# Pair sums of the hidden activations made in place from two loaded blocks, and ten weight sums moved to the second gate loop

## The reference, cut to what matters

```python
# first block, phase E of the kernel
f = (silu(h @ w_ffn_gate) * (h @ w_ffn_up)) @ w_ffn_down
x = x + rms_norm(f, norm_ffn_post)
# second block, phase H of the kernel
h = x @ w_up                      # 1024 x 5632
h = causal_conv3(h, conv_w) + conv_b
a, g = split(h, 2)
out = (silu(g) * a) @ w_down      # then residual and the final norm
```

## Time and profile before

| what | us |
|---|---|
| median of three runs | 3157.57 |
| lowest and highest run | 3152.23, 3159.49 |
| the profiled execution | 3161.4 |
| its span | 3159.7 |
| PE busy | 2939.5 (93%) |
| DVE busy | 1897.9 (60%) |
| ACT busy | 1315.3 (42%) |
| POOL busy | 725.5 (23%) |

### The profile page before, as it was taken

The page is one execution under the profiler, slowest core; times in us unless marked ns, Lnnn a source line. Parts: engine busy times, 40 slices in busy tenths (PEclk is TensorE's granted clock), DMA queues, the critical chain, the costliest instruction groups (busy, mean ns, idle before and its releaser), DMA issues.

```text
span 3159.7 us, 41058 instructions
## 1 busy us (share of the span) xinstructions
PE 2939.5 (93%) x14905; PEld 2400.7 (76%) x14905; DVE 1897.9 (60%) x2684; ACT 1315.3 (42%) x2136; POOL 725.5 (23%) x645
## 2 busy tenths in 40 slices
PE   8989999999989798999999999999979899988898
PEld 6767778778868576788777887788867677767687
DVE  3546565565675647666556574555744776777656
ACT  3531441541542435233224453555644444333444
POOL 3211121221231301334662001333510000243200
PEclk8999999999999999999999999999989999999999
DMA  4256356356342562555458564557663344556765
GB/s 138 71 155 141 122 145 160 99 147 149 97 123 61 194 227 80 144 160 139 144 159 285 181 220 137 142 184 183 172 203 135 101 114 115 163 152 199 250 200 194
DMA packets 330037, 488.32 MB, mean 155 GB/s; under 512 B 18818, under 2 KB 214160, under 8 KB 329888
## 3 DMA queue, kind: packets, MB, share of 16 engines
q1 hardware_dynamic: 276064, 298.16, 30.3%
q0 software_dynamic: 48016, 171.37, 20.1%
q10 hardware_dynamic: 5808, 16.79, 1.8%
HBM read 379.24 MB, written 199.29 MB: 183 GB/s over the span
## 4 chain that ended last, share of the span: by engine, by line
PE 66%; DVE 13%; DMA 8%; ACT 6%; issue 3%; POOL 3%; SPq 1%; DVEq 0%; ACTq 0%; POOLq 0%
PE PS L671 19%; PE PS L2528 15%; PE PS L2548 12%; PE PS L377 5%; PE PS L1504 2%; DMA pair_hidden<-hidden_scratch 1%; DVE gate_up L2422 1%; PE PS L1470 1%; PE PS L1398 1%; DMA down_raw<-up_sums 1%; PE PS L1387 1%; DVE w_L L2374 1%; DMA sb_branch<-u_scratch 1%; PE PS L3218 1%; PE PS L3205 1%
## 5 line engine op out<-in xcount | busy, mean ns | idle before, releaser
L671 PE MATMUL PS<-hH,w_H 128*128 128x512 f32 x1072 | 453.5, 423 | 22.8 <-DVE w_L L334 12.5
L671 PE MATMUL PS<-hH,w_L 128*128 128x512 f32 x1072 | 426.2, 398 | 0.0
L671 PE MATMUL PS<-hL,w_H 128*128 128x512 f32 x1072 | 424.3, 396 | 0.0
L334 DVE TENSOR_TENSOR w_L<-w_raw,w_H 128x1024 fp32r<-128x1024 f32 x107 | 133.7, 1250 | 218.6 <-ACT w_H L329 218.4
L671 PEld LDWEIGHTS PS<-hH,w_H 128*128 128x128 f32 x1072 | 207.1, 193 | 68.4 <-issue 12.3
L2528 PE MATMUL PS<-hH,fast_w 128*128 128x512 f32 x672 | 232.6, 407 | 23.6 <-ACT gate_up L2300 21.2
L671 PEld LDWEIGHTS PS<-hH,w_L 128*128 128x128 f32 x1072 | 204.9, 191 | 46.6
L671 PEld LDWEIGHTS PS<-hL,w_H 128*128 128x128 f32 x1072 | 206.4, 193 | 35.8 <-issue 1.7
L2528 PE MATMUL PS<-sums,w_H 128*128 128x512 f32 x672 | 212.3, 398 | 8.4 <-DVE gate_up L2422 8.2
L2528 PEld LDWEIGHTS PS<-hH,fast_w 128*128 128x128 f32 x672 | 129.5, 193 | 61.8 <-ACT gate_up L2300 25.0
L2824 POOL TENSOR_SCALAR prob<-prob,den_inverse 128x128 f32<-128x128 f32 (+3 forms) x64 | 110.3, 1723 | 234.0 <-DVE den_inverse L3034 233.7
(11 more groups left out here) (477 smaller groups left out, 6758.6 us busy)
## 6 DMA issues: line engine op xcount, KB each, us to landing
up_sums<-in_w_up POOLq DMA_DIRECT2D x24, 1408.0 KB, 10.3
w_raw<-in_w_in SPq DMA_DIRECT2D x62, 512.0 KB, 4.6
u_scratch<-unit_staged SPq DMA_DIRECT2D x50, 512.5 KB, 5.2
hidden_scratch<-hidden SPq DMA_DIRECT2D x44, 512.0 KB, 5.0
pair_sums<-pair_sum POOLq DMA_DIRECT2D x22, 1024.0 KB, 5.6
turned_raw<-pair_sums SPq DMA_DIRECT2D x88, 256.0 KB, 3.0
turned_raw<-down_sums SPq DMA_DIRECT2D x88, 256.0 KB, 4.1
down_raw<-up_sums SPq DMA_DIRECT2D x42, 512.0 KB, 6.6
```

The lines of the kernel that those rows point to most:

```text
L334: e.tensor_tensor(wL[c % 2][:, :, :], raw[c % 2][:, :, :], f32(wH[c % 2][:, :, :]), ALU.subtract).then_inc(s_wL, 1)
L671: mm = e.matmul(PS[:, f.bank(o, half), :], w[:, k0 + k, :], x[:, k, half * HALF:(half + 1) * HALF], start=(k == 0 and j == 0), stop=(k == ...
```

## The change

**Pair sums.** POOL no longer reads `hidden`. It waits until tile 11 + p is stored, loads both tiles p and 11 + p from DRAM into `pair_sum`, one turn later makes the four sums there in place, in a chain in which each waits for the one before, and stores all 2048 columns. The order of the four in the buffer differs, so `DOWN_A` names them in another order. The waits of ACT (`up_start`) and DVE (`tile_hidden`) on `pair_summed` are gone. The memory of `pair_hidden` stays as a pad.

**Order on POOL.** In a turn of the second half POOL now does: the sums of the pair before, then the wait for the next weights, the store of the pair, (in E) the four weight sums, and then the two loads of the next pair. Before it was: wait for the weights, store, load, (E) weight sums, pair sums.

**Slots of the down loop.** The first nine steps take slots 0, 1, 2, 9, 10, 7, 3, 4, 5 (before 0, 1, 2, 9, 10, 3, 4, 5, 6) and the ring of nine behind them runs in another order, so that the slot in `silu_out` and `hidden` is first used at step 13 (before 8) and that in `pair_sum` at step 17 (before 10). The store of the last `hidden` tile is issued behind the load of step 11 (before 8). The check that tiles are stored moves from step 11 to steps 20 and 21.

**Weight sums in DRAM.** F now issues 5 of the 64 parts (before 16), G 3, and the last 10 are issued in the first eleven turns of H's gate loop.

```diff
-                ("pair_loaded", "EH", 16 * NG), ("pair_summed", "EH", 8 * NG), ("pair_stored", "EH", 16 * NG),
+                ("pair_loaded", "EH", 32 * NG), ("pair_summed", "EH", 4 * NG), ("pair_stored", "EH", 16 * NG),
...
-        DOWN_A = ((HIDDEN, 0, 0), (HIDDEN, NG, 0), (SUMS, 1), (SUMS, 0), (SUMS, 3), (SUMS, 2), (HIDDEN, NG, 1))
+        DOWN_A = ((HIDDEN, 0, 0), (HIDDEN, NG, 0), (SUMS, 0), (SUMS, 3), (SUMS, 2), (SUMS, 1), (HIDDEN, NG, 1))
...
-        slot_no = lambda n: (0, 1, 2, NSLOT, NSLOT + 1)[n] if n < 5 else (n - 2) % NSLOT
+        SLOT_FIRST, SLOT_RING = (0, 1, 2, NSLOT, NSLOT + 1, 7, 3, 4, 5), (0, 1, 2, 7, 6, 3, 4, 5, 8)
+        slot_no = lambda n: SLOT_FIRST[n] if n < NSLOT else SLOT_RING[(n - NSLOT) % NSLOT]
...
-            if n == NG:
-                e.wait_ge(sem("fast_stored"), since(tag, "fast_stored", 16 * FT))
+            if n in (2 * NG - 2, 2 * NG - 1):
+                e.wait_ge(sem("fast_stored"), since(tag, "fast_stored", 16 * (n + 1)))
...
-            elif n in (5, 6):
+            elif n == 5:
+                e.wait_ge(sem("down_L"), since(tag, "down_L", 6))
+            elif n in (6, 7):
                 e.wait_ge(sem("fast_P"), since(tag, "fast_P", 7 * NW))
-            elif n == 7:
+            elif n == 8:
                 e.wait_ge(sem("hidden"), since(tag, "hidden", FT))
-            elif n == 8:
+            elif n == 13:
                 e.wait_ge(sem("fast_stored"), since(tag, "fast_stored", 16 * FT))
-                e.wait_ge(sem("pair_summed"), since(tag, "pair_summed", 8 * NG))
-            elif n == 9:
-                e.wait_ge(sem("pair_summed"), since(tag, "pair_summed", 8 * NG))
-                e.wait_ge(sem("down_L"), since(tag, "down_L", 6))
-            elif n == 10:
+            elif n == 17:
                 e.wait_ge(sem("pair_stored"), since(tag, "pair_stored", 16 * NG))
...
-                if n == 8:
+                if n == 11:
                     store(None, NW, FT - 1)
...
+            def pair_sums(p):
+                e.wait_ge(sem("pair_loaded"), since(tag, "pair_loaded", 32 * p + 32))
                 summed = sem("pair_summed")
+                done = lambda n: e.wait_ge(summed, since(tag, "pair_summed", 4 * p + n))
+                a_lo, a_hi, b_lo, b_hi = (pair_sum[:, i, :] for i in range(4))
+                e.tensor_tensor(b_hi, a_hi, b_hi, ALU.subtract).then_inc(summed, 1)
                 done(1)
+                e.tensor_tensor(a_hi, a_lo, a_hi, ALU.subtract).then_inc(summed, 1)
                 done(2)
+                e.tensor_tensor(a_lo, a_lo, b_hi, ALU.subtract).then_inc(summed, 1)
+                done(3)
+                e.tensor_tensor(b_lo, b_lo, a_lo, ALU.subtract).then_inc(summed, 1)
...
+            def pair_load(p):
+                e.wait_ge(sem("fast_stored"), since(tag, "fast_stored", 16 * (NG + p + 1)))
+                if p:
+                    e.wait_ge(sem("pair_stored"), since(tag, "pair_stored", 16 * p))
+                for i in range(2):
+                    e.dma_start(pair_sum[:, 2 * i:2 * i + 2, :], h_scr[:, i * NG + p, :].rearrange("p (n c) -> p n c", n=2))\
+                        .then_inc(sem("pair_loaded"), 16)
...
             for t in range(NW):
+                if t > NG:
+                    pair_sums(t - NG - 1)
                 if t < NW - 1:
                     tile_loaded(t + 2)
-                if t < NG and tag == "E":
+                if t < NG:
                     weight_sums_next(parts, 1)
-                if t == NG:
-                    e.wait_ge(sem("hidden"), since(tag, "hidden", 2))
                 if t > NG:
-                    pair_store(t - 1)
-                if t >= NG:
-                    pair_load(t)
+                    pair_store(t - NG - 1)
                 if tag == "E" and t < NW - 1:
                     weight_sums(1, t)
                 if t >= NG:
-                    pair_sums(t)
+                    pair_load(t - NG)
...
@@ up_start (ACT, H) and tile_hidden (DVE, E)
-                e.wait_ge(sem("pair_summed"), own("pair_summed", tag, 4 * c + 3, it, 4))
...
@@ pool_F
-                if G % 4 == 2:
+                if G % 13 == 6:
                     weight_sums_next(parts, 1)
@@ pool_H
+            pool_ffn(e, "H", "G", UH, parts)
             assert next(parts, e) is e
-            pool_ffn(e, "H", "G", UH, parts)
```

More of the change, by code:

```diff
@@ L272, in build @@
                 op_pair = sb("down_operands_pair", [P, 8, HALF], F32R, s1)
-            pair_sum, pair_h, raw_first = T("pair_sum", (P, 4, HALF)), T("pair_hidden"), T("down_raw_first", (P, 2, HALF))
+            pair_sum, pad_E, raw_first = T("pair_sum", (P, 4, HALF)), T("pad_e"), T("down_raw_first", (P, 2, HALF))
             cvt = T("conv_columns", (P, 16))
@@ L2178, in pair_sums @@
                 summed = sem("pair_summed")
-                done = lambda n: e.wait_ge(summed, own("pair_summed", tag, n, it, 4))
-                s1, s2, s3, s4 = (pair_sum[:, i, :] for i in range(4))
-                e.tensor_tensor(s1, pair_h[:, hi], hfE[:, hi], ALU.subtract).then_inc(summed, 1)
+                done = lambda n: e.wait_ge(summed, since(tag, "pair_summed", 4 * p + n))
+                a_lo, a_hi, b_lo, b_hi = (pair_sum[:, i, :] for i in range(4))
+                e.tensor_tensor(b_hi, a_hi, b_hi, ALU.subtract).then_inc(summed, 1)
@@ L2193, in pair_load, with pair_store @@
-            def pair_load(it):
-                e.dma_start(pair_h[:, :], h_scr[:, it - NG, :]).then_inc(sem("pair_loaded"), 16)
+                e.tensor_tensor(a_lo, a_lo, b_hi, ALU.subtract).then_inc(summed, 1)
+                done(3)
+                e.tensor_tensor(b_lo, b_lo, a_lo, ALU.subtract).then_inc(summed, 1)
+            def pair_store(p):
+                e.wait_ge(sem("pair_summed"), since(tag, "pair_summed", 4 * p + 4))
+                e.dma_start(pair_scr[:, :, p, :].rearrange("n p c -> p n c"), pair_sum[:, :, :])\
+                    .then_inc(sem("pair_stored"), 16)
@@ L2199, in tile_loaded @@
                     e.wait_ge(sem("fast_T"), since(tag, "fast_T", 32 * j))
-            e.sem_inc(sem("pair_summed"), 4 * NG)
             if tag == "E":
@@ L2218, in pool_ffn @@
                 if t >= NG:
-                    pair_sums(t)
-            pair_store(NW - 1)
-            pair_load(NW)
-            pair_sums(NW)
-            pair_store(NW)
+                    pair_load(t - NG)
+            for p in range(NW - NG, NG):
+                pair_sums(p - 1)
+                pair_store(p - 1)
+                pair_load(p)
+            pair_sums(NG - 1)
+            pair_store(NG - 1)
             e.wait_ge(sem("fast_P"), since(tag, "fast_P", 7 * NW))
```

6 lines of the change are left out of this document (removed).

## The result

| kernel | median us | lowest, highest | runs |
|---|---|---|---|
| before | 3159.31 | 3152.23, 3159.60 | 5 |
| changed | 3138.91 | 3132.76, 3143.70 | 5 |

The account below looks back on a forecast made before the run. PE was busy 93% of the span, so gains could come only from its idle time: 9.0 + 7.7 + 19.5 + 8.5 + 1.0 - 1.5 = 44.2 us off, giving 3113 us; own range 3103 to 3121, wider range 3098 to 3138.

Parts of the forecast that it names:

- Point 3: H's gate loop: ACT no longer waits for POOL, pair sums hold one tap, 0.9 us a turn; gain 19.5 us.
- sums against taps: Rival, H's gate loop: four pair sums hold two taps and two low parts, 3.2 us a turn; 3133 us, chance 0.15.
- Points 2 and 4: From gate loop into down loop: the step 11 wait shrinks to 0.6 us; gain 7.7 us in E, 8.5 in H.
- point 4: H, into the down loop: 11.1 us less 2.5 lost to held DVE operations; gain 8.5 us, bounds 3 and 11.6.
- Point 1: E's gate loop: pair sums move to where DVE mostly waits, shortening the weights' ring; gain 9.0 us, bounds 0 and 11.4.
- POOL's ring: Rival, E's gate loop: loads landing in 8 us or more make it 21.2 us; E's 9.0 go, 3122 us, chance 0.12.
- the bound of 11.4: E's gate loop, second half: upper bound of the gain in us, the sum of PE's eight waits there.
- Points 5 to 8: Down loops otherwise: nothing; F: gain 1 us; G: nothing; H's first half with ten weight-sum parts: loss 1.5 us.
- Pair loads at nothing: Gate loops: the extra MB read each turn, issued when the turn's weights have landed, costs nothing.

Follow-up runs that it names:

- short sums: The changed kernel with its four pair sums working on 8 of each 512 columns, loads, stores and order kept: 3104.17 us, ratio 0.9829 to before.

## Why the prediction was wrong

**Point 3 failed, in its last step.** The working was right up to the time of the sums: ACT's wait for POOL went, POOL was on nobody's path, the loads landed before the next turn and the sums began with it. Then it priced what they meet there at one tap of 0.92 us, a mean between no tap and two. They meet four operations of VectorE's for each pair. The sums of one pair begin with the weights' issue (2725.86 for 2725.82) and hold both up taps, the column copy and `hidden`; PE waits 2.63 us. The loads of the next pair land 19.9 us behind that issue, as worked out, but by then the turn is late, so that its sums, from 2745.70, hold the gate half's second tap, two low parts and the first up tap. The next weights are issued at 2751.94, 26.1 us behind the last; the turns after that take 20.1, 26.3, 20.4, 22.4 and 25.9. I had named this as the rival "sums against taps", at 3.2 us for a turn and a chance of 0.15; it came out at 2.9, and short sums take away all of it. A turn of over 22.5 us was also the first thing that the prediction named as a sign of being wrong. What the profile had said for the rival, a chain without a gap from the fourth sum on, was the better evidence than the share of the turn that the sums fill.

The Trainium skill (SBUF — State Buffer, section "SBUF: two separate sides") says that a VectorE operation with two SBUF inputs and a GpSimd operation that reads SBUF exclude each other for a whole instruction. The runs agree in kind: every held operation has two SBUF inputs or is the copy, VectorE's sums with a PSUM input keep 0.69 us beside a pair sum, and POOL's sums are held in turn, up to 2.17 us for 1.29. Of a copy the Trainium skill (SBUF — State Buffer, section "Who interferes with whom") says that it can run in a mode that takes the shared ports too. The estimate that I drew from it, two held taps or 2.6 us and a gain of 4.2, was nearer than the value I took (the gate loop gained 2.1).

**Points 2 and 4** took the wait at step 11 to be ACT's wait for the last pair's store and left 0.6 us of it. What was late next was in the code that I had read: the taking of group 0 is queued behind step 16's high part. The loads of steps 14 to 16 come through a ring of four raw slots, whose pace I had not worked out. 3.29 and 6.47 us stayed, and went when the taking moved three steps forward. The slower matmuls behind the wait stayed with it. In H the sums of pair 9 hold the last tile's taps besides, as forecast: with short sums the wait is 3.13 and step 5's wait of 1.45 is gone. Gained 2.9 and 3.0 for 7.7 and 8.5. (11.1 - 2.5 in point 4 is 8.6; that changes nothing.)

**Point 1 was right** in its size, 10.6 us for 9.0, and only in part in its mechanism. POOL's ring is short enough: in seven of eight turns the pair sums end 1.0 us or more before ACT starts on the next weights, in one 0.2 behind. But the sums do not fall into idle time of VectorE. In E's second half they hold `hidden` and a low part (1555 ns for 699), 1.95 us a turn together. `hidden`, 1500:1665, in the changed kernel, and under it with short sums:

```profile
L2414 DVE TENSOR_TENSOR hidden<-gate_up,silu_out 128x1024 f32<-128x1024 f32 x8 | 18.5, 2317 | 0.0
```

```profile
L2414 DVE TENSOR_TENSOR hidden<-gate_up,silu_out 128x1024 f32<-128x1024 f32 x9 | 11.0, 1223 | 0.0
```

Of these 1.95 us some 0.4 reach the turn: it is 19.9, and 19.44 with short sums. The same kind of loss as in H meets slack here. PE's own pace is those 19.44 and not 19.70, which was a mean with slower first turns in it, so that the bound of 11.4 was too low: with short sums this stretch gains 13.6.

**Points 5 to 8** held within 1.5 us: the down loops are unchanged, F (from its first product to G's) takes 422.7 for 422.6, so that the gain of 1 is none, and the first half of H runs at 20.00 for 20.05 us a turn with the ten weight sums in it, so that the loss of 1.5 is none. "Pair loads at nothing" held for this change, and only for where it puts them.

## What to carry to other kernels

When a wait is taken away, ask what the engine that was waited for does in the freed time and what it then runs beside: here a turn was 3.2 us too long, and 2.9 of them were given back as operations of another engine that got longer, and only their durations showed it. Sum those excesses over a turn and compare them with what the turn is too long; if they agree, move the work to where the held operations have slack (1.95 us held in E's turn cost 0.4), and check that the DMAs behind it don't land on a burst. A long wait for a copy out of PSUM may be only the copy's place in its engine's program.

## What the runs showed of the hardware

- A copy of 128x8 took 172 to 176 ns alone and 582 on the mean, up to 0.99 us, beside POOL's sums: a held operation pays for its neighbour's length and not its own.
- One sum's 1.3 us is not the most that an operation can lose, as the prediction had it: in seven turns of E's second half the first low part took 2.28 or 2.29 us for 0.68, beside POOL's issue of the pair's store (0.80) and its first weight sum (1.30). It did so with short pair sums too; which of the two holds it, or both, is open.
- With two loads of 512 KB from POOL issued 1 us behind 1792 KB of SP's, the last parts of the latter landed in 9.8 us in place of 6.3; with those loads issued 14.4 us or more behind, in 6.3 to 6.7.
- TensorE's granted clock fell behind some of its waits and not behind others. Windows of the changed kernel (busy us of PE, PEld, DVE, ACT, POOL, granted clock, DMA share, GB/s), one turn without long waits and two with them:

```profile
2507.00:2527.00 20.00, 19.66 (x86) 15.61 (x84) 14.12 (x19) 8.30 (x12) 0.58 (x1) 1.00 0.62 189
2700.00:2745.90 45.90, 40.53 (x168) 31.97 (x167) 33.63 (x36) 16.85 (x24) 17.13 (x15) 0.96 0.62 194
```

  Behind the wait of 6.47 us the clock was 0.50 from 2942 to 2946, the lower of its two levels (1.2 GHz), and twelve matmuls took 4.66 us in place of 2.88. Around the ends of two waits of 2.63 us it was 0.75 (2730:2734) and 0.72 (2778:2782) on the mean; the next two matmuls took 1.22 us the first time and 0.73, as elsewhere, the second. Behind waits of 2.21 and 2.35 us it stayed at 1.00 (2822:2830, 2892:2900).
